# Two chunk-quads of the RWKV-7 recurrence interleaved hop by hop, with the copy of U double-buffered

## The reference, cut to what matters

```python
def step(state, inp):
    r_t, w_t, k_t, v_t, kk_t, a_t = inp
    sa = jnp.einsum('bhvk,bhk->bhv', state, -kk_t)
    state = (state * w_t[:, :, None, :]
             + sa[..., None] * (kk_t * a_t)[:, :, None, :]
             + v_t[..., None] * k_t[:, :, None, :])
    return state, jnp.einsum('bhvk,bhk->bhv', state, r_t)
_, y = lax.scan(step, s0, xs)
...  # group norm over each head, scale, bonus, gate
out = (yn + bonus.reshape(bsz, t, D_MAIN)) * g.astype(f32)
```

## Time and profile before

| | us |
|---|---|
| median of the runs | 3019.81 |
| the profiled execution, its own time | 3014.53 |
| its span, first to last instruction | 3012.7 |
| recurrence, first U to the last y | 380.3 to 828.1 |
| PE busy of the whole span | 2819.7 (94%) |

### The profile page before, as it was taken

How to read it: one execution, slowest core, us unless ns; L and a number is a source line. 1 busy time by engine, 2 the same in 40 slices (tenths; PEclk the granted TensorE clock), 3 DMA queues, 4 the chain that set the end, 5 groups by cost and what they waited for, 6 DMA issues and landing times. The chain is left out here.

```text
span 3012.7 us, 55312 instructions
## 1 busy us (share of the span) xinstructions
PE 2819.7 (94%) x23253; PEld 2270.3 (75%) x23253; DVE 1566.9 (52%) x2143; ACT 1063.1 (35%) x1858; POOL 1167.2 (39%) x1121
## 2 busy tenths in 40 slices
PE   7999788888879999999999999988889999999998
PEld 5888567777657788888887777756667788888887
DVE  6233456666452844445224777867653754455222
ACT  3111333333232533333003766545442433333000
POOL 6354023333222544444433554432012544444431
PEclk9999799999989999999999999999999999999999
DMA  5332200000033132224423233342122232225321
GB/s 201 109 105 84 98 17 24 24 24 32 3 105 105 44 110 84 84 84 143 139 79 102 56 99 98 111 149 85 64 85 77 63 112 84 84 84 171 108 69 65
DMA packets 265422, 261.19 MB, mean 87 GB/s; under 512 B 9367, under 2 KB 221453, under 8 KB 264025
## 3 DMA queue, kind: packets, MB, share of 16 engines
q1 hardware_dynamic: 258520, 235.50, 24.7%
q10 hardware_dynamic: 6176, 22.13, 2.1%
q0 software_dynamic: 480, 0.03, 0.0%
HBM read 186.80 MB, written 70.83 MB: 86 GB/s over the span
## 5 line engine op out<-in xcount | busy, mean ns | idle before, releaser
L304 POOL TENSOR_TENSOR w_lo_b<-w_raw_b,w_hi_b 128x512 fp32r<-128x512 f32 (+1 forms) x500 | 665.2, 1332 | 516.9 <-ACT w_hi_b L336 503.3
L386 PE MATMUL ps<-b_hi,w_hi_b 128*128 128x512 f32 x1540 | 608.5, 395 | 13.1 <-issue 9.0
L386 PE MATMUL ps<-b_lo,w_hi_b 128*128 128x512 f32 x1540 | 601.1, 390 | 0.0
L386 PE MATMUL ps<-b_hi,w_lo_b 128*128 128x512 f32 x1540 | 601.0, 390 | 0.0
L386 PEld LDWEIGHTS ps<-b_hi,w_hi_b 128*128 128x128 f32 x1540 | 290.2, 188 | 79.2 <-issue 14.1
L386 PEld LDWEIGHTS ps<-b_lo,w_hi_b 128*128 128x128 f32 x1540 | 290.3, 188 | 63.4 <-issue 3.6
L386 PEld LDWEIGHTS ps<-b_hi,w_lo_b 128*128 128x128 f32 x1540 | 290.0, 188 | 60.8
L336 ACT ACTIVATE w_hi_b<-w_raw_b 128x512 fp32r<-128x512 f32 x330 | 206.0, 627 | 249.5 <-DVE w_raw_b L323 126.3
L300 POOL CAST w_hi_b<-w_raw_b 128x384 fp32r<-128x384 f32 (+2 forms) x170 | 99.5, 585 | 492.5 <-PE ps L358 307.8
L358 PE MATMUL ps<-b_hi,w_hi_b 128*128 128x512 f32 x784 | 244.4, 393 | 11.7 <-DVE b_lo L2735 9.0
L358 PE MATMUL ps<-b_lo,w_hi_b 128*128 128x512 f32 x784 | 243.8, 392 | 0.0
(11 more groups left out here) (334 smaller groups left out, 5241.7 us busy)
## 6 DMA issues: line engine op xcount, KB each, us to landing
w_raw_b<-in_w_gate_up SPq DMA_DIRECT2D x88, 512.0 KB, 4.2
act_dram<-x_res SPq DMA_DIRECT2D x44, 512.0 KB, 6.0
stage<-act_dram ACTq DMA_DIRECT2D x32, 512.0 KB, 3.5
w_raw_b<-in_w_down SPq DMA_DIRECT2D x32, 384.0 KB, 3.7
w_raw_a<-in_a_w_in SPq DMA_DIRECT2D x23, 512.0 KB, 4.7
u_dram<-evac_a SPq DMA_DIRECT2D x23, 512.0 KB, 3.0
w_raw_b<-in_w_down SPq DMA_DIRECT2D x32, 320.0 KB, 3.1
w_raw_b<-in_w_out SPq DMA_DIRECT2D x16, 512.0 KB, 6.5
```

Of the source, the lines that this page charges most:

```text
L304: nc.gpsimd.tensor_tensor(self.wlo[:, r, 0:n, :], source, self.whi[:, r, 0:n, :].bitcast(F32), ALU.subtract).then_inc(self.w_lo, 1)
L386: mm = self.nc.tensor.matmul(self.ps[:, bank, :], w[:, r, k, :], h[:, block, k, :], start=(start and k == 0 and a == 0 and h is self.bh), ...
```

## The change

Two steps are in flight. In hop l of loop iteration s, PE forms the U of one step and, right behind it, the XX of the other; each rests on the hop before. The functions `u_at` and `xx_at` say which: odd hops take U of step s (levels 1, 2, 3) and XX of step s-1 (levels 3, 4, 5); even hops take U of step s-1 (levels 4, 5) and XX of step s (levels 1, 2). The loop runs S + 2 = 26 iterations instead of 25, and the tail belongs to step s-2. U goes to bank 6, `um` and `lab` get two buffers, `xx` gets three, r gets three. All side products share bank 7, so their halves j = 0, 1 go to different hops. The sums of squares go to bank 6 beside U; the copy of U takes them along (272 columns instead of 256 in two hops of a window), and POOL reads them there, which takes two small operations off DVE. POOL also takes over the last two operations of the group norm (`group_bonus`, `group_out`, 128x1024 each, once a pair but for the last). The copy of the chunk decays moves from DVE to ACT.

```diff
-            xx = sb("xx", [P, 2, 2, 4, C])
-            lak, lab = sb("lak", [P, 4, C]), sb("lab", [P, 4, C])
+            xx = sb("xx", [P, 3, 2, 4, C])
+            lak, lab = sb("lak", [P, 4, C]), sb("lab", [P, 2, 4, C])
-            um = sb("um", [P, 4, C])
+            um = sb("um", [P, 2, 4 * C + 16])
+            def u_at(s, l):
+                n, level = (s, (l + 1) // 2) if l % 2 else (s - 1, l // 2 + 3)
+                return (n, level) if 0 <= n < S else None
+            def xx_at(s, l):
+                n, level = (s - 1, (l + 5) // 2) if l % 2 else (s, l // 2)
+                return (n, level) if 0 <= n < S else None
...
+                def sums_work(s, l):
+                    w, r = window(s), place(s, l)
+                    if r in (5, 6) and 2 <= w < PAIRS:
+                        kk_sums(w, r - 5)
+                    elif r in (11, 16) and 2 <= w <= PAIRS:
+                        norm_sums(w - 2, (r - 11) // 5)
...
+                def inverse_u(n, l):
+                    pe.wait_ge(u_copied, u_count[n, l] - 1)
+                    pe.wait_ge(join_done, join_count[n, l])
+                    if l == 1:
+                        pe.wait_ge(x0, n + 1)
+                    else:
+                        pe.wait_ge(xx_added, xx_count[n, l - 1])
+                    ...
+                def inverse_xx(n, l):
+                    pe.wait_ge(u_copied, u_count[n, l])
+                    pe.wait_ge(xx_added, xx_count[n, l] - 1)
+                    pe.wait_ge(x0, n + 1)
+                    ...
-                for s in range(S + 1):
+                for s in range(S + 2):
                     for l in range(1, LEVELS + 1):
+                        now_xx, now_u = xx_at(s, l), u_at(s, l)
+                        o, n = s - 2, s + 1
+                        if now_u:
+                            pe.wait_ge(u_copied, u_count[now_u] - 1)
+                            sums_work(s, l)
+                            inverse_u(*now_u)
+                        if now_xx:
+                            inverse_xx(*now_xx)
+                        if o >= 0 and l == 5:
+                            tail(o, 3)
+                        if l == 1 and s < S:
+                            piece(s, 5)
+                        if o >= 0 and l in (1, 2, 4):
+                            tail(o, {1: "bars", 2: "gh", 4: 1}[l])
+                        side_work(s, l)
+                        if n < S and l in (1, 2, 4, 5):
+                            piece(n, {1: 2, 2: 3, 4: 0, 5: 4}[l])
+                        if o >= 0 and l >= 3:
+                            tail(o, {3: 0, 4: 2, 5: "y"}[l])
+                        if n < S and l == 4:
+                            piece(n, 1)
...
+                def group_bonus(p):
+                    pool.wait_ge(gn_formed, 2 * p + 2)
+                    yp = y[:, p % 2, :]
+                    nc.gpsimd.tensor_tensor(yp, yp, bonus[:, p % 3, :], ALU.add).then_inc(gn_bonus, 1)
+                def group_out(p):
+                    pool.wait_ge(gn_bonus, p + 1)
+                    pool.wait_ge(g_act, 2 * p + 2)
+                    nc.gpsimd.tensor_tensor(self.X[:, p, :], y[:, p % 2, :], g[:, p % 2, :], ALU.mult).then_inc(pair_done, 1)
...
+                    if w < PAIRS and r == 16:
+                        keep_decay(w)
-                        elif r == 11:
-                            group_square(w - 2)
+                        if r in (10, 15):
+                            group_square(w - 2, (r - 10) // 5)
```

552 lines of the change are left out of this document (298 added, 254 removed).

## The result

The changed kernel takes 3040.4 us (median of 4, 3035.2 to 3053.6), the kernel before 3020.2 in the same runs. The ratio is 1.0065 (95% interval 1.0046 to 1.0084): slower by 0.65%, where I had forecast 1.3% faster. The profiled execution took 3035.2 us, with a span of 3033.2.

The account below looks back on a forecast made before the run. PE, busy 94% of the span, was taken as the bound, with gains only from its waits. Gains of 25.5, 12 and 7.5 less 6.5, with small extras, made 40 us: 2980 us median, eight-in-ten range 2961 to 3003.

Parts of the forecast that it names:

- The floor: Steps 3 to 18: PE's own work without waits, put at 62.6 us per window of four steps.
- The round trips: Steps 3 to 18: waits for copy and add go, five late places cost 5.2 us per window; 298.5 to 273 us.
- waits for sums of squares: Waits ahead of a U for ACT's squares: 1.1 us at r = 5, 1.1 at r = 11, 0.7 at r = 16.
- U behind the bare hop r = 7: Hop without side work, only a state step of 0.12 us: the next U waits about 0.95 us.
- The state steps: At r = 12, PE wants the second state step at 4.9 us, DVE finishes at 5.7: a wait of 0.9 us.
- The sign of being wrong: Among the signs named for a wrong forecast: PE's busy time itself grows, which nothing in the prediction foresaw.
- Steps 19 to 22: Late steps of the recurrence: from 64.6 us to 57, a gain of 7.5 us.
- Start and end: Steps 0 to 2 gain 12 us; step 23 and the last tail lose 6.5 us.
- Rival 1: Round trips stay in part: 120 hops lose 0.2 us each, 24 us, giving 3004 us; chance 0.15.
- Rival 2: DVE's add comes late for the U behind it, so hops grow; 0.7 us per hop gives 3068 us; chance 0.06.
- Rival 3: POOL's 10 operations of 2.5 us slow DVE beside them: about 12 us less gain, 2992 us; chance 0.08.
- Rival 4: The late places vanish because one wait covers the next: 21 us more gain, 2959 us; chance 0.11.

Follow-up runs that it names:

- e5: Changed kernel with state steps moved, ACT's squares earlier, and GpSimd's x0 addition held back behind two DVE products: 3009.0 us, 0.9957 of the kernel before.
- e2: Changed kernel with ACT squaring the keys one hop earlier and y ahead of its copies: 3023.3 us, 1.0008 of the kernel before.
- e4: Changed kernel with matmuls of constant tiles into unused columns filling three kinds of PE waits: 3029.8 us, 1.0025 of the kernel before.
- e14: 16 small matmuls, a quarter packet, added to the best version (state steps moved, squares earlier, x0 held back, transfers late; 3002.1 us): 3011.6 us.
- e16: 48 small matmuls, three quarters of a packet, added to the best version (state steps moved, squares earlier, x0 held back, transfers late): 3030.9 us.
- e7: Changed kernel with state steps moved, squares earlier, and the next stage's transfers issued only at the recurrence's end: 3010.9 us, 0.9965 of the kernel before.
- e12: Best version (state steps moved, squares earlier, x0 held back, transfers late) with 32 gh matmuls replaced by 8 wider ones, results not the reference's: 2989.9 us.
- e13: Kernel before the change with 32 gh matmuls replaced by 8 wider ones, results not the reference's: 3012.3 us, 0.9968 of the kernel before.
- e11: Best version (state steps moved, squares earlier, x0 held back, transfers late) with the two 128x1024 group operations back on DVE: 3002.8 us.

## Why the prediction was wrong

**The floor was right.** I had PE's own work as 62.6 us per window, 250.4 in four, and 2 more for a decay product. The waits view of the changed kernel has 32 waits of 23.4 us and 13 "issue" pauses of 14.0. With 0.2 hidden behind each, the estimate of the forecast, these are 29.8 and 16.6, and the clock cost 19.1. 318.0 - 29.8 - 16.6 - 19.1 = 252.5, as forecast; that it fits to 0.1 is luck, with a clock rounded to 0.01. (The same sum on the kernel before, with its 63 waits and pauses of 29.7 us by that view and its one drop of the clock, gives 254.5.) So the 45 us between 273 and 318 are 9 of waits too few (29.8 where I had 20.8), 16.6 of pauses, and 19.1 of clock.

**The step that failed is "The round trips".** It added five late places, 5.2 us per window, to a floor at full clock, and took it that nothing else would come up once the waits for copy and add were gone.

- Its waits for sums of squares were sized well: 11.6 us forecast for r = 5, 11 and 16 in four windows, 10.1 in the view. U behind the bare hop r = 7 was sized too high (3.8, against 1.2 for all waits for the add).
- The state steps were forecast late at one place, 0.9 x 4 = 3.6 us; the view has 10.7. I took DVE's operations at the durations of before, and the r-k product took 2.18 instead of 1.28. e5 shows it.
- The clock was priced at the start and at the end only. It is the largest single term in the middle: taking away waits of 10 us gave 17 (e2), and behind filled waits the clock stayed up (e4). The sign of being wrong that I had named, a PE whose busy time grows (281 for 267), is what it looks like.
- The pauses were in no step. e14 to e16 show where they sit, e7 and e12 two things that change them: other traffic, and the number of instructions. That they cost less before because PE then waited in nearly every hop, and the fetch caught up in that time, fits the 60 packets in both kernels and 3.9 us against 14.0, and the edit of e12 and e13 being worth 15 us in the one and 5 in the other without the clock; but it was not tested by itself, and by the times alone e13 did not bear it out.

**Steps 19 to 22** failed in the same way: five "issue" pauses of 5.2 us and 3.1 us at sums and state steps, where I had 2.5 in all. **Start and end** came as forecast in kind, at 50.3 for 46.5 and 32.6 for 32.5.

**The rivals.** Rival 1, small delays at every hop: no, U waits for the add in 4 places of 80 hops. Rival 2, the exchange loses because the add comes late: no, for the same reason; the kernel is slower, but through another mechanism, and my 0.05 for slower rested on this one alone. Rival 3, contention: its mechanism is real, and e5 prices it at about 7 us (known to 6), but it works through x0 and the joins, which now run beside two large DVE products, and not through the two operations moved to GpSimd (e11). The rule of the Trainium skill, GPSIMD Engine Reference, section 8: a DVE instruction with two SBUF inputs contends with GpSimd for SBUF. The trace agrees, with 2.18 against 1.27 us; b_decay, beside joins, had 1.40 against 1.22. Rival 4: no, more places were late, not fewer. None of them had the clock, though the earlier trace rows showed it at half at both ends of the stage.

## What to carry to other kernels

When round trips are taken out of a tuned stream, price each wait that stays by what the granted clock does behind it (here 17 to 23 us for 10 us of waits), and look first for the late operation that a hop waits for, not for a better place of the waiter. Read the durations of engines that share a memory path again for the new overlaps: an operation that was alone may not be alone any more. And a stream of short matmuls has a limit that the waits of before can hide: count instructions per us, keep large transfers away from the dense places, and before you credit or blame an edit of PE's code with 10 us, run it again with the code shifted by part of a packet.

## What I had not expected of the hardware

- A wait of 0.9 us was followed by 3.4 us at 0.50 of the clock (450.80 to 454.20). Of twelve waits of 0.9 to 1.7 us eight were followed by such a drop, and before the change one of four of 1.8 us.
- PE stops for 0.2 to 4.4 us at some of the edges of its 16 KB instruction packets (13 of 60 in steps 3 to 18 of the changed kernel), in runs of matmuls that depend on nothing. The pause ends 0.8 to 1.65 us after the packet has landed, stands at fixed numbers of instructions from the program's start (8614 to 8616 matmuls in four kernels), and is longer with 3 MB of loads beside it (1.9 to 4.4 us in six kernels, against 1.1 to 1.4 in four).
- An f32 matmul of the program is two matmuls and two weight loads in PE's stream (64 gave x128 more of each).
- DVE's product of two SBUF tiles takes 2.18 us beside GpSimd's x0 and join, 1.27 alone, and the join 1.71 against 0.73: both sides lose.
